# A triangular inverse by doubling: the fine levels kept 32 columns wide per head, with VectorE block transposes in place of TensorE's

## The chip, the cores and the metric

One core of one Trainium2 chip. The metric is the device time of one execution in microseconds (us), the median of several runs.

## What is computed

The program runs two transformer blocks on 256 tokens of width 1024: a first block with mixture-of-experts weights (most of the time), and a second one with forgetting attention and a gated delta rule. The change lies in the delta rule. The reference solves, per head and chunk, a unit lower triangular system:

```
A = jnp.where(tri_strict, einsum(kb, kc) * decay, 0.0)
lhs = A + jnp.eye(C)
sol = lax.linalg.triangular_solve(lhs, concatenate([vc * bc, kb * exp(gc)]), lower=True, unit_diagonal=True)
```

The kernel works with chunks of 128 tokens (two chunks, `t` = 0, 1), 8 heads in two groups of four (`hg` = 0, 1, `HG` = 4), all in 32-bit floats. Instead of solving, it builds the inverse of `lhs` itself, and multiplies with it afterwards.

## The kernel before

Everything of interest stands in `phase_c`, which writes each engine's instructions out by hand, in order, with semaphores between engines. TensorE writes into eight PSUM banks in rotation; the class `Banks` plans which bank each product gets (`banks.plan`, L1852 to L1855), TensorE claims it, the reader takes and releases it, and `banks.moved` waits for such a release.

**The inverse by doubling.** X is the inverse of the block diagonal part of `lhs` with blocks of size 2^l, XT its transpose. Level l joins pairs of blocks: with ATm, the transposed A masked to the off-diagonal squares that level l joins (mask `lm[:, l]`, with a minus sign in it), the step is X <- X + X (A masked) X. Level 0 needs no product. Levels 1 to 6 run in a loop (TensorE L2398 to L2426). One level is, for both chunks t, with four heads each:

- POOL masks A into ATm (L2095), 128x512 numbers per chunk.
- TensorE: t1 = ATm times X, four products of 128x128 by 128x128 (L2407), and from level 2 on a transpose of X, four more (L2413).
- ScalarE copies t1 out of PSUM (L2002) and the transposed X into XT (L2005).
- TensorE: XT times T1, four products (L2425).
- VectorE adds the result to X, at the last level to XT (L2252).

A 32-bit product of 128x128 by 128x128 appears in the trace as two passes, each a weight load (PEld, LDWEIGHTS) and a MATMUL; a transpose is one pass. So a level has 32 passes of products and 8 of transposes.

**What stands around it.** Ahead of the loop VectorE forms XT of level 0 (L2243), TensorE transposes it (`x1`, L2394) and ScalarE copies it to X (L1994). These lie between the projections `fv` and `gz` (`rows`, L1745 to L1752). Behind the loop come the attention logits `lo` (L2436 to L2445) and the products with XT (L2458). Projections run as three products of a high and a low part of the weights; ScalarE makes the high part (L183), VectorE and POOL in turn the low part (L186), four 128x1024 units ahead, in between their other work, where the code says `units.ahead`. SyncE loads a new 2 MB piece of weights into one of two slots once all low parts of the piece two before it are made (L70). POOL also masks the attention weights of the delta rule (L2087), and at the start of the phase it builds the level masks `lm` and other constants, of which `negmask` (L2072) is the last.

Of the kernel before, what the change touches and what calls it, by code (L numbers as in the profile page):

```python
# [31 lines left out]
ALU = mybir.AluOpType  # L32
ACT = mybir.ActivationFunctionType
AX = mybir.AxisListType

P = 128
# [1757 lines left out]
def phase_c(nc, A, sem, sb, ring, banks, k, env):  # L1794
# [20 lines left out]
    ATm, T1 = work[:, 0], work[:, 1]  # L1815
# [27 lines left out]
    for hg in range(2):  # L1843
# [6 lines left out]
                   ("fv", hg, 0), ("fv", hg, 1), *[("x1", hg, t) for t in range(NT)],  # L1850
                   ("gz", hg, 0), ("gz", hg, 1))
        for l in range(1, LEVELS):  # L1852
            for t in range(NT):
                banks.plan(("t1", hg, l, t), *([("tr", hg, l, t)] if l > 1 else []))
            banks.plan(*[("xx" if l < LEVELS - 1 else "xt", hg, l, t) for t in range(NT)])  # L1855
# [12 lines left out]
    with nc.Block() as block:  # L1868
# [18 lines left out]
        def _(act):  # L1887
# [48 lines left out]
            for hg in range(2):  # L1936
# [55 lines left out]
                for t in range(NT):  # L1992
                    bank = banks.take(act, ("x1", hg, t))
                    banks.release(act.copy(X[:, t], heads(bank)), ("x1", hg, t))  # L1994
                for t in range(NT):
# [51 lines left out]
        def _(g):  # L2047
# [6 lines left out]
            for l in range(LEVELS):  # L2054
                if l == 1:
# [10 lines left out]
                                      pattern=[[2 * b, m], [0, b]], channel_multiplier=-1))  # L2066
            mask_plain = vb[:, 0, 0, :]
# [6 lines left out]
            for hg in range(2):  # L2074
                u0 = UNITS_GROUP * hg
                units.ahead(g, "low1", u0 + 20)
                g.wait_ge(sem("kk"), 4 * hg + 4)
                for l in range(LEVELS):
                    if l == 1:
                        units.ahead(g, "low1", u0 + 24)  # L2080
                    if l in (4, 5):
                        units.ahead(g, "low1", u0 + 24 + 2 * (l - 3))
                    if l in (2, 3):

                        for h in (2 * l - 4, 2 * l - 3):
                            banks.moved(g, ("kq", hg, h))
                            g.tensor_tensor(attnT[:, :, h, :], attnT[:, :, h, :],  # L2087
                                            tri[:, :].unsqueeze(1).to_broadcast([P, NT, P]), ALU.mult)\
                                .then_inc(sem("attn_masked"), 1)
                    for t in range(NT):  # L2090
                        if l > 1:
                            banks.done(g, ("t1", hg, l - 1, t))
                        if l == 1:
                            g.wait_ge(sem("x1T"), NT * hg + t + 1)
                        g.tensor_tensor(heads(ATm[:, t, :]), AT[:, t], lm[:, l, :].unsqueeze(1).to_broadcast([P, HG, P]),  # L2095
                                        ALU.mult).then_inc(sem("ATm"), 1)
# [3 lines left out]
        def _(v):  # L2100
# [73 lines left out]
            for hg in range(2):  # L2174
# [65 lines left out]

                for t in range(NT):
                    v.wait_ge(sem("ATm"), 2 * LEVELS * hg + t + 1)
                    v.tensor_tensor(XT[:, t], heads(ATm[:, t, :]), ident[:, :].unsqueeze(1).to_broadcast([P, HG, P]),  # L2243
                                    ALU.add).then_inc(sem("x1T"), 1)
                units.ahead(v, "low0", UNITS_GROUP * hg + 28)
                for l in range(1, LEVELS):
                    for t in range(NT):
                        w, buf = ("xx", X) if l < LEVELS - 1 else ("xt", XT)
                        bank = banks.take(v, (w, hg, l, t))
                        if w == "xt":  # L2250
                            banks.moved(v, ("tr", hg, l, t))
                        banks.release(v.tensor_tensor(buf[:, t], buf[:, t], heads(bank), ALU.add), (w, hg, l, t))  # L2252
# [44 lines left out]
        def _(pe):  # L2297
# [41 lines left out]
            for hg in range(2):  # L2339
# [50 lines left out]
                for t in range(NT):  # L2390
                    pe.wait_ge(sem("x1T"), NT * hg + t + 1)
                    bank = banks.claim(pe, ("x1", hg, t))
                    for h in range(HG):
                        last = pe.transpose(bank[:, h * P:(h + 1) * P], XT[:, t, h, :], ident[:, :])  # L2394
                    banks.filled(last, ("x1", hg, t))
# [403 lines left out]
```

## Time and profile before

| | |
|---|---|
| median of 3 runs | 1648.52 us (1648.29 to 1649.6) |
| the profiled execution | 1648.02 us, its span 1646.3 us |
| TensorE (PE) busy | 99% of the span |
| weight loads (PEld) | 57% |
| VectorE, ScalarE, POOL | 37%, 29%, 18% |
| granted TensorE clock, mean | 0.998 |
| level loop, group 0 / group 1 | 1146.51 to 1174.31 us / 1285.10 to 1312.89 us |

Starts are given in us from the span's start. In a timeline a row's first number is its start, the second its length, and a number in brackets is how long the engine had been idle before it, with what released it. Rows of one line are merged, so that "x8" is eight instructions. The granted clock is a share of full speed: 1.00 is 2.4 GHz, 0.50 is 1.2 GHz. A MATMUL's end is modelled and contains the pipeline's latency, so lengths of MATMULs overlap; the distance between starts tells what one costs.

### The profile page before, as it was taken

The numbers are of one execution on the slowest core, as the hardware profiler recorded it, in microseconds if no ns is written. First come the engines' busy times: TensorE is split into PE (matmuls) and PEld (weight loads), VectorE is DVE, ScalarE is ACT, GpSimd is POOL, SyncE is SP. The second block draws the span as 40 slices with busy tenths as digits, with TensorE's granted clock in tenths as the row PEclk, the third lists the DMA queues.
The fourth block names the chain that finished last, engine by engine and source line by source line (L and its number), as shares of the span: only waits on it lengthen the run. The fifth ranks groups of instructions, "written<-read, shape, count | busy, mean of one in ns | idle before, by whom it ended". The sixth has DMA issues, their size and how long they took to land. (4 is left out here: it accounts for less than half of the span.)

```text
span 1646.3 us, 22758 instructions
## 1 busy us (share of the span) xinstructions
PE 1624.4 (99%) x9272; PEld 946.4 (57%) x9272; DVE 613.7 (37%) x1144; ACT 475.8 (29%) x695; POOL 302.4 (18%) x192
## 2 busy tenths in 40 slices
PE   9999999999999999999999999999999999999998
PEld 8843333333333333333333333698998999999986
DVE  7743212112121212121121211675485244468852
ACT  5421110111111111111011111574555454454443
POOL 3500000000000000000000000535333624445552
PEclk9999999999999999999999999999999999999999
DMA  9698999999999999999999999353133215456552
GB/s 350 221 367 338 428 427 426 428 427 426 428 426 427 429 426 427 426 428 428 428 428 428 428 428 422 125 179 128 53 123 134 103 52 195 166 166 203 167 192 102
DMA packets 92919, 507.67 MB, mean 308 GB/s; under 512 B 8987, under 2 KB 32584, under 8 KB 68264
## 3 DMA queue, kind: packets, MB, share of 16 engines
q1 hardware_dynamic: 92696, 506.00, 76.1%
q8 instruction: 61, 1.00, 0.3%
q10 hardware_dynamic: 144, 0.52, 0.1%
q14 instruction: 18, 0.15, 0.0%
HBM read 505.46 MB, written 1.05 MB: 308 GB/s over the span
## 5 line engine op out<-in xcount | busy, mean ns | idle before, releaser
L186 POOL TENSOR_TENSOR low<-ring,high 128x1024 fp32r<-128x1024 f32 x81 | 199.6, 2465 | 1262.8 <-ACT high L183 1262.7
L1593 PE MATMUL ps<-ring,x 128*64 128x512 f32 x1536 | 337.5, 594 | 1.8 <-DMA ring<-in_w_up 1.8
L1593 PEld LDWEIGHTS ps<-ring,x 128*64 128x64 f32 x1536 | 108.0, 137 | 227.5 <-issue 222.4
L183 ACT CAST high<-ring 128x1024 fp32r<-128x1024 f32 x162 | 168.2, 1047 | 201.4 <-PE ps L1727 125.5
L1720 PE MATMUL ps<-hTh,high 128*128 128x256 f32 x800 | 198.8, 285 | 2.4 <-DVE hTl L633 1.9
L1721 PE MATMUL ps<-hTl,high 128*128 128x256 f32 x800 | 197.6, 284 | 0.0
L1626 PE MATMUL ps<-ring,x 128*64 128x512 f32 x752 | 171.7, 598 | 0.0
L186 DVE TENSOR_TENSOR low<-ring,high 128x1024 fp32r<-128x1024 f32 x81 | 111.1, 1371 | 146.7 <-ACT high L183 146.6
L1720 PEld LDWEIGHTS ps<-hTh,high 128*128 128x128 f32 x800 | 153.9, 192 | 4.2 <-issue 3.8
L1721 PEld LDWEIGHTS ps<-hTl,high 128*128 128x128 f32 x800 | 154.0, 192 | 0.0
L1466 DVE TENSOR_SCALAR hT<-ps 128x512 f32<-128x512 f32 x32 | 22.1, 692 | 295.8 <-PE ps L1593 295.8
L1593 PE MATMUL ps<-extra,x 128*64 128x512 f32 x512 | 113.8, 594 | 0.0
L1727 PE MATMUL ps<-hTh,low 128*128 128x256 f32 x784 | 110.8, 284 | 0.0
L1626 PEld LDWEIGHTS ps<-ring,x 128*64 128x64 f32 x752 | 49.8, 136 | 103.9 <-issue 103.9
L1727 PEld LDWEIGHTS ps<-hTh,low 128*128 128x128 f32 x784 | 101.9, 193 | 0.0
L1418 DVE TENSOR_TENSOR x<-ps,g 128x512 f32<-128x512 f32 x33 | 22.8, 692 | 204.3 <-PE ps L1559 204.3
L1531 ACT COPY hT<-ps 128x512 f32<-128x512 f32 x32 | 18.8, 586 | 261.5 <-PE ps L1626 261.5
L1526 ACT COPY gpickT<-ps 128x256 f32<-128x256 f32 x32 | 11.9, 372 | 251.5 <-PE ps L1606 251.5
L1522 ACT ACTIVATE hT<-hT 128x512 f32<-128x512 f32 x32 | 20.1, 630 | 220.9 <-DVE hT L1466 220.9
L1472 DVE TENSOR_SCALAR hT<-ps 128x512 f32<-128x512 f32 x32 | 22.1, 691 | 155.5 <-PE ps L1593 155.5
L1593 PEld LDWEIGHTS ps<-extra,x 128*64 128x64 f32 x512 | 36.0, 137 | 75.1 <-issue 74.4
L1568 PE MATMUL ps<-hT,gpickT 64*128 64x512 f32 x264 | 65.6, 615 | 0.7 <-ACT hT L1531 0.7
(465 smaller groups left out, 2181.7 us busy)
## 6 DMA issues: line engine op xcount, KB each, us to landing
ring<-in_w_down SPq DMA_DIRECT2D x52, 2048.0 KB, 20.5
ring<-in_w_gate SPq DMA_DIRECT2D x48, 2048.0 KB, 18.2
ring<-in_w_up SPq DMA_DIRECT2D x48, 2048.0 KB, 18.5
ring<-in_w_in SPq DMA_DIRECT2D x23, 2048.0 KB, 8.2
extra<-in_w_gate SPq DMA_DIRECT2D x16, 2048.0 KB, 18.9
extra<-in_w_up SPq DMA_DIRECT2D x16, 2048.0 KB, 17.5
extra<-in_w_down SPq DMA_DIRECT2D x14, 2048.0 KB, 21.0
ring<-in_w_up SPq DMA_DIRECT2D x22, 1024.0 KB, 7.4
```

What stands on the lines that cost most here:

```text
L183: eng.copy(hi, self.raw(u)).then_inc(self.sem("high_split"), 1)
L186: eng.tensor_tensor(lo, self.raw(u), hi.bitcast(F32), ALU.subtract).then_inc(self.sem(who + "_split"), 1)
L1418: bank_free(v.tensor_tensor(xg[:, :, :, :], bank.rearrange("p (c h j) -> p c h j", c=4, h=2), gains, ALU.mult), G_)
L1466: bank_free(v.tensor_scalar(gt[:, :], bank, 7.0, None, ALU.min), GATE)
L1472: bank_free(v.tensor_scalar(up[:, :], bank, 7.0, -7.0, ALU.min, ALU.max), UP)
L1522: act.activation(sg[:, :], gt[:, :], ACT.Sigmoid, scale=1.702).then_inc(sem("sig"), 1)
L1568: last = pe.matmul(total(t, h), gpickT[h * CAP:(h + 1) * CAP, t, :], y[h * CAP:(h + 1) * CAP, :], start=False, stop=final)
L1593: last = pe.matmul(bank[h * CAP:(h + 1) * CAP, :], xg[:, c, kh, :], w[:, c, h * 512:(h + 1) * 512], start=False, stop=kh == 1 and c == 3)
L1626: last = pe.matmul(bank[h * CAP:(h + 1) * CAP, :], aT[:, c, kh, :], w[:, c, h * 512:(h + 1) * 512], start=False, stop=kh == 1 and c == 3)
L1720: pe.matmul(out, wh[:, w], xh[:, c, :], start=c == 0, stop=False)
L1721: last = pe.matmul(out, wh[:, w], xl[:, c, :], start=False, stop=False)
L1727: last = pe.matmul(out, wl[:, c * P:(c + 1) * P], xh[:, c, :], start=False, stop=c == KC - 1)
```

## The change

X keeps, for each head, only 32 columns while the blocks are at most 32 wide (`Xc`, 32 columns per head: row block b of it holds the diagonal 32x32 block b). With that, levels 1 to 4 work on 32 columns per head in place of 128. The product is taken with the full mask `below` of all levels under 5, and what does not belong to level l is masked away on the product by VectorE (`below_c`). XT stays 128 wide (block diagonal) and gets its new blocks from Xc by four VectorE transposes of 32x(4x32) per chunk. Level 5 works on 32 columns, then X is widened to 64 columns (`Xw`), and level 6 writes only the missing quarter of XT: at level 5 VectorE copies, per chunk, twice 32 rows into Xw and twice 32 rows into XT, at level 6 once 64 rows into XT. POOL makes 8 masks per group in place of 14. The `x1` transposes and the ones in the loop (`tr`) are gone.

Buffers and constants:

```
-    ATm, T1 = work[:, 0], work[:, 1]
+    near, far = work[:, 0], work[:, 1]
+    R = 32
+    Xw, Xc, Tc, Tw = X[:, :, :, 0:2 * R], X[:, :, :, 2 * R:3 * R], X[:, :, :, 3 * R:], X[:, :, :, 2 * R:]
+    below = sb("below", [P, P])
+    below_c = sb("below_c", [P, 4, R])
+    odd_row = sb("odd_row", [P, 1])
+    FINE = 5
+    XT_STEPS, AT_STEPS = 4 + NT * (FINE - 1), 8
+    def blocks(odd=None):
+        return [slice(b, b + R) for b in range(R if odd else 0, P, R if odd is None else 2 * R)]
```

ScalarE: no copies of `x1`, `t1` only at levels 5 and 6.

```
-                for l in range(1, LEVELS):
+                for l, to, w in ((FINE, Tc, R), (FINE + 1, Tw, 2 * R)):
                     for t in range(NT):
+                        if l == FINE:
+                            banks.moved(act, ("xx", hg, l - 1, t))
+                            act.copy(Xw[:, t, :, 0:R], Xc[:, t])
+                            act.activation(Xw[:, t, :, R:], Xc[:, t], ACT.Copy, scale=odd_row[:, 0:1])
                         bank = banks.take(act, ("t1", hg, l, t))
-                        banks.release(act.copy(T1[:, t, :], bank), ("t1", hg, l, t))
-                        if l > 1:
-                            bank = banks.take(act, ("tr", hg, l, t))
-                            banks.release(act.copy(XT[:, t], heads(bank)), ("tr", hg, l, t))
+                        last = act.copy(to[:, t], bank[:, 0:HG * w].rearrange("p (h n) -> p h n", h=HG))
+                        banks.release(last, ("t1", hg, l, t))
```

POOL, at the start of the phase, ahead of `negmask`, and per group:

```
+            chain(g.tensor_tensor(below[:, :], lm[:, 0, :], lm[:, 1, :], ALU.add))
+            for l in range(2, FINE):
+                chain(g.tensor_tensor(below[:, :], below[:, :], lm[:, l, :], ALU.add))
...
+                def masked(to, t, mask):
+                    g.tensor_tensor(heads(to[:, t, :]), AT[:, t], mask.unsqueeze(1).to_broadcast([P, HG, P]), ALU.mult)\
+                        .then_inc(sem("ATm"), 1)
+                for t in range(NT):
+                    masked(far, t, lm[:, 0, :])
+                for t in range(NT):
+                    masked(near, t, below[:, :])
+                units.ahead(g, "low1", u0 + 24)
+                for t in range(NT):
+                    g.wait_ge(sem("x1T"), XT_STEPS * hg + 2 * t + 1)
+                    masked(far, t, lm[:, FINE, :])
+                for h in range(HG):
+                    banks.moved(g, ("kq", hg, h))
+                    g.tensor_tensor(attnT[:, :, h, :], attnT[:, :, h, :],
+                                    tri[:, :].unsqueeze(1).to_broadcast([P, NT, P]), ALU.mult)\
+                        .then_inc(sem("attn_masked"), 1)
+                for t in range(NT):
+                    banks.done(g, ("t1", hg, FINE - 1, t))
+                    masked(near, t, lm[:, FINE + 1, :])
+                units.ahead(g, "low1", u0 + 28)
```

VectorE (levels 5 and 6 as told above):

```
+                if hg == 0:
+                    v.wait_ge(sem("consts2"), 1)
+                    for rows in blocks():
+                        v.transpose(below_c[rows, :, :], lm[rows, 1:FINE, rows])
+                    chain(v.tensor_reduce(odd_row[:, :], lm[:, FINE, :], AX.X, ALU.add))
+                    chain(v.tensor_scalar(odd_row[:, :], odd_row[:, :], 1.0 / R, 1.0, ALU.mult, ALU.add))
                 for t in range(NT):
-                    v.wait_ge(sem("ATm"), 2 * LEVELS * hg + t + 1)
-                    v.tensor_tensor(XT[:, t], heads(ATm[:, t, :]), ident[:, :].unsqueeze(1).to_broadcast([P, HG, P]),
+                    v.wait_ge(sem("ATm"), AT_STEPS * hg + t + 1)
+                    v.tensor_tensor(XT[:, t], heads(far[:, t, :]), ident[:, :].unsqueeze(1).to_broadcast([P, HG, P]),
                                     ALU.add).then_inc(sem("x1T"), 1)
+                    v.wait_ge(sem("x1T"), XT_STEPS * hg + 2 * t + 1)
+                    for rows in blocks():
+                        last = v.transpose(Xc[rows, t], XT[rows, t, :, rows])
+                    last.then_inc(sem("x1T"), 1)
                 units.ahead(v, "low0", UNITS_GROUP * hg + 28)
-                for l in range(1, LEVELS):
+                def fine(bank):
+                    return bank[:, 0:HG * R].rearrange("p (h n) -> p h n", h=HG)
+                for l in range(1, FINE):
                     for t in range(NT):
-                        w, buf = ("xx", X) if l < LEVELS - 1 else ("xt", XT)
-                        bank = banks.take(v, (w, hg, l, t))
-                        if w == "xt":
-                            banks.moved(v, ("tr", hg, l, t))
-                        banks.release(v.tensor_tensor(buf[:, t], buf[:, t], heads(bank), ALU.add), (w, hg, l, t))
+                        bank = banks.take(v, ("t1", hg, l, t))
+                        last = v.scalar_tensor_tensor(Tc[:, t], fine(bank), -1.0,
+                                                      below_c[:, l - 1, :].unsqueeze(1).to_broadcast([P, HG, R]),
+                                                      ALU.mult, ALU.mult)
+                        banks.release(last, ("t1", hg, l, t))
+                    for t in range(NT):
+                        bank = banks.take(v, ("xx", hg, l, t))
+                        banks.release(v.tensor_tensor(Xc[:, t], Xc[:, t], fine(bank), ALU.add), ("xx", hg, l, t))
+                        banks.moved(v, ("xx", hg, l, t))
+                        for rows in blocks():
+                            last = v.transpose(XT[rows, t, :, rows], Xc[rows, t])
+                        last.then_inc(sem("x1T"), 1)
```

TensorE:

```
                 for l in range(1, LEVELS):
+                    left, n = (near, 2) if l < FINE else (far, 4) if l == FINE else (near, 6)
+                    right, w = (Xc, R) if l <= FINE else (Xw, 2 * R)
                     for t in range(NT):
-                        pe.wait_ge(sem("ATm"), 2 * LEVELS * hg + 2 * l + t + 1)
+                        pe.wait_ge(sem("ATm"), AT_STEPS * hg + n + t + 1)
                         if l == 1:
-                            banks.moved(pe, ("x1", hg, t))
+                            pe.wait_ge(sem("x1T"), XT_STEPS * hg + 2 * t + 2)
                         else:
                             banks.moved(pe, ("xx", hg, l - 1, t))
                         bank = banks.claim(pe, ("t1", hg, l, t))
                         for h in range(HG):
-                            last = pe.matmul(bank[:, h * P:(h + 1) * P], ATm[:, t, h * P:(h + 1) * P], X[:, t, h, :],
+                            last = pe.matmul(bank[:, h * w:(h + 1) * w], left[:, t, h * P:(h + 1) * P], right[:, t, h, :],
                                              start=True, stop=True)
                         banks.filled(last, ("t1", hg, l, t))
-                        if l > 1:
-                            bank = banks.claim(pe, ("tr", hg, l, t))
-                            for h in range(HG):
-                                last = pe.transpose(bank[:, h * P:(h + 1) * P], X[:, t, h, :], ident[:, :])
-                            banks.filled(last, ("tr", hg, l, t))
                     for t in range(NT):
                         banks.moved(pe, ("t1", hg, l, t))
-                        if l > 1:
-                            banks.moved(pe, ("tr", hg, l, t))
-                        w = "xx" if l < LEVELS - 1 else "xt"
-                        bank = banks.claim(pe, (w, hg, l, t))
-                        for h in range(HG):
-                            a, b = XT[:, t, h, :], T1[:, t, h * P:(h + 1) * P]
-                            if w == "xt":
-                                a, b = b, a
-                            last = pe.matmul(bank[:, h * P:(h + 1) * P], a, b, start=True, stop=True)
-                        banks.filled(last, (w, hg, l, t))
+                        if l <= FINE:
+                            if l > 1:
+                                pe.wait_ge(sem("x1T"), XT_STEPS * hg + 4 + NT * (l - 2) + t + 1)
+                            bank = banks.claim(pe, ("xx", hg, l, t))
+                            for h in range(HG):
+                                last = pe.matmul(bank[:, h * R:(h + 1) * R], XT[:, t, h, :], Tc[:, t, h, :],
+                                                 start=True, stop=True)
+                            banks.filled(last, ("xx", hg, l, t))
+                        if l == FINE:
+                            bank = banks.claim(pe, ("xt", hg, l, t))
+                            for b in (0, 2 * R):
+                                for h in range(HG):
+                                    last = pe.matmul(bank[b:b + R, h * R:(h + 1) * R], Tc[:, t, h, :],
+                                                     XT[:, t, h, b + R:b + 2 * R], start=True, stop=True)
+                            banks.filled(last, ("xt", hg, l, t))
+                        if l > FINE:
+                            banks.moved(pe, ("xt", hg, FINE, t))
+                            bank = banks.claim(pe, ("xt", hg, l, t))
+                            for h in range(HG):
+                                last = pe.matmul(bank[0:2 * R, h * w:(h + 1) * w], Tw[:, t, h, :], XT[:, t, h, 2 * R:],
+                                                 start=True, stop=True)
+                            banks.filled(last, ("xt", hg, l, t))
```

## Rows read from the trace of the kernel before

**Rows 1.** The page, busy time of each engine over the whole span.
```profile
PE 1624.4 (99%) x9272; PEld 946.4 (57%) x9272; DVE 613.7 (37%) x1144; ACT 475.8 (29%) x695; POOL 302.4 (18%) x192
```
**Rows 2.** Busy time by stretch: PE, PEld, DVE, ACT, POOL, clock, DMA share, GB/s.
```profile
1146.51:1174.31 27.80, 27.35 (x235) 26.70 (x233) 7.57 (x12) 13.79 (x26) 18.51 (x14) 1.00 0.22 77
```
**Rows 3.** Timeline of level 3 of group 0: start, length, engine, line.
```profile
1155.70 0.97 PEld L2407 LDWEIGHTS ps<-X,work 128*128 128x128 f32 x8
...
1156.90 0.59 ACT L2002 COPY work<-ps 128x512 f32<-128x512 f32 x1 [2.21 <-PE ps L2407]
...
1158.36 1.98 PEld L2425 LDWEIGHTS ps<-work,XT 128*128 128x128 f32 x16
...
1159.56 0.69 DVE L2252 TENSOR_TENSOR X<-X,ps 128x512 f32<-128x512 f32 x1 [2.92 <-PE ps L2425]
...
1160.32 0.97 PEld L2407 LDWEIGHTS ps<-X,work 128*128 128x128 f32 x8
```
**Rows 4.** Timeline, the x1 transposes of group 0 and the next weight load.
```profile
1134.73 1.03 PEld L2394 LDWEIGHTS ps<-ident,XT 128*128 128x128 f32 x8
...
1135.73 0.19 PEld L1745 LDWEIGHTS ps<-high,hTh 128*128 128x128 f32 x1
```
**Rows 5.** Timeline of the router: products with 32 moving columns, and a reader.
```profile
119.70 0.52 PEld L1274 LDWEIGHTS ps<-fold,part_sums 128*128 128x128 f32 x4 [1.01 <-ACT part_sums L843]
...
120.44 0.22 DVE L1048 TENSOR_TENSOR lg<-ps,brt 128x64 f32<-128x64 f32 x1 [2.44 <-PE ps L1274]
...
123.82 0.30 PEld L1285 LDWEIGHTS ps<-mask,ones 128*128 128x128 f32 x2
...
124.04 0.30 PEld L1286 LDWEIGHTS ps<-mask,ustrict 128*128 128x128 f32 x2
...
124.39 0.09 PEld L1287 LDWEIGHTS ps<-mask,ones 128*1 128x1 f32 x2
```
**Rows 6.** Groups of instructions by line and shape: busy in all, mean ns of one.
```profile
L990 DVE TENSOR_TENSOR extra<-ps,extra 128x128 f32<-128x128 f32 x4 | 1.1, 273 | 0.0
L2087 POOL TENSOR_TENSOR xn<-xn,tri 128x256 f32<-128x256 f32 x8 | 5.7, 734 | 0.0
```
**Rows 7.** Timeline of VectorE: one pair with a wait between, one without.
```profile
1177.78 0.41 DVE L2257 TENSOR_REDUCE fmax<-ps 128x1 f32<-128x256 f32 x1
1178.22 0.17 DVE L2258 TENSOR_SCALAR fmax<-fmax 128x2 f32<-128x2 f32 x1
...
1181.58 0.28 DVE L2262 TENSOR_SCALAR work<-work,fsum 128x128 f32<-128x128 f32 x1
1181.78 0.35 DVE L2263 TENSOR_SCALAR work<-work,fsum 128x256 f32<-128x256 f32 x1
```
**Rows 8.** Timeline: low-part splits and the products that wait for them, a load.
```profile
1065.16 4.75 POOL L186 TENSOR_TENSOR low<-ring,high 128x1024 fp32r<-128x1024 f32 x2
...
1070.10 0.28 PE L1727 MATMUL ps<-hTh,low 128*128 128x256 f32 x1
...
1128.71 1.21 DVE L186 TENSOR_TENSOR low<-ring,high 128x1024 fp32r<-128x1024 f32 x1
...
1130.84 2.40 POOL L186 TENSOR_TENSOR low<-ring,high 128x1024 fp32r<-128x1024 f32 x1 [3.36 <-ACT high L183]
...
1137.67 0.62 PE L1752 MATMUL ps<-low,hTh 128*128 128x512 f32 x2
...
1162.10 0.37 SPq L70 DMA_DIRECT2D ring<-in_w_in  x1
```
**Rows 9.** Busy time by stretch around 1245 us (columns as in rows 2).
```profile
1241.90:1245.30 3.40, 3.40 (x18) 2.48 (x18) 2.16 (x8) 3.38 (x5) 0.39 (x1) 0.99 0.53 149
1245.30:1248.70 3.40, 3.40 (x19) 3.40 (x18) 2.50 (x4) 3.39 (x10) 0.00 (x0) 0.51 1.05 405
```
**Rows 10.** Timeline, TensorE in these two stretches.
```profile
1242.15 0.18 PEld L2367 LDWEIGHTS ps<-row_high,sel 8*128 8x128 f32 x1 [0.76 <-issue]
...
1246.77 1.82 PEld L1727 LDWEIGHTS ps<-hTh,low 128*128 128x128 f32 x8
...
```

More of the change, by code:

```diff
@@ L1849, in phase_c @@
                    *[(w, hg, t) for w in ("kt", "vt") for t in range(NT)],
-                   ("fv", hg, 0), ("fv", hg, 1), *[("x1", hg, t) for t in range(NT)],
+                   ("fv", hg, 0), ("fv", hg, 1),
                    ("gz", hg, 0), ("gz", hg, 1))
         for l in range(1, LEVELS):
+            banks.plan(*[("t1", hg, l, t) for t in range(NT)])
             for t in range(NT):
-                banks.plan(("t1", hg, l, t), *([("tr", hg, l, t)] if l > 1 else []))
-            banks.plan(*[("xx" if l < LEVELS - 1 else "xt", hg, l, t) for t in range(NT)])
+                banks.plan(*[(w, hg, l, t) for w in (["xx"] * (l <= FINE) + ["xt"] * (l >= FINE))])
         banks.plan(*[("lo", hg, h) for h in range(HG)], ("u0", hg), ("wT", hg), ("st", hg), ("o0", hg), ("u1", hg),
@@ L1992, in _ @@
                 for t in range(NT):
-                    bank = banks.take(act, ("x1", hg, t))
-                    banks.release(act.copy(X[:, t], heads(bank)), ("x1", hg, t))
-                for t in range(NT):
                     ahead(u0 + 24 + (3, 4)[t])
@@ L2077, in _ @@
                 g.wait_ge(sem("kk"), 4 * hg + 4)
[L2078 to L2090, printed above, removed]
-                        if l > 1:
[L2092 to L2096, printed above, removed]
+                def masked(to, t, mask):
[18 more added lines that the diff above has]
+                units.ahead(g, "low1", u0 + 28)
             units.ahead(g, "low1", UNITS_E + 11)
@@ new lines, in _ @@
+                for t in range(NT):
+                    bank = banks.take(v, ("xx", hg, FINE, t))
+                    for rows in blocks(True):
+                        last = v.tensor_copy(Xw[rows, t, :, 0:R], fine(bank)[rows])
+                    banks.release(last, ("xx", hg, FINE, t))
+                    bank = banks.take(v, ("xt", hg, FINE, t))
+                    for b in (0, 2 * R):
+                        last = v.tensor_copy(XT[b:b + R, t, :, b + R:b + 2 * R], fine(bank)[b:b + R])
+                    banks.release(last, ("xt", hg, FINE, t))
@@ L2254, in _ @@
+                for t in range(NT):
+                    bank = banks.take(v, ("xt", hg, FINE + 1, t))
+                    wide = bank[0:2 * R, 0:HG * 2 * R].rearrange("p (h n) -> p h n", h=HG)
+                    banks.release(v.tensor_copy(XT[0:2 * R, t, :, 2 * R:], wide), ("xt", hg, FINE + 1, t))
                 for h in range(HG):
@@ L2389, in _ @@
                 both_t(u0 + 20, "fv", hg)
-                for t in range(NT):
-                    pe.wait_ge(sem("x1T"), NT * hg + t + 1)
-                    bank = banks.claim(pe, ("x1", hg, t))
-                    for h in range(HG):
-                        last = pe.transpose(bank[:, h * P:(h + 1) * P], XT[:, t, h, :], ident[:, :])
-                    banks.filled(last, ("x1", hg, t))
                 both_t(u0 + 24, "gz", hg)
                 for l in range(1, LEVELS):
+                    left, n = (near, 2) if l < FINE else (far, 4) if l == FINE else (near, 6)
+                    right, w = (Xc, R) if l <= FINE else (Xw, 2 * R)
                     for t in range(NT):
-                        pe.wait_ge(sem("ATm"), 2 * LEVELS * hg + 2 * l + t + 1)
+                        pe.wait_ge(sem("ATm"), AT_STEPS * hg + n + t + 1)
                         if l == 1:
-                            banks.moved(pe, ("x1", hg, t))
+                            pe.wait_ge(sem("x1T"), XT_STEPS * hg + 2 * t + 2)
                         else:
@@ L2415, in _ @@
                     for t in range(NT):
                         banks.moved(pe, ("t1", hg, l, t))
-                        if l > 1:
-                            banks.moved(pe, ("tr", hg, l, t))
-                        w = "xx" if l < LEVELS - 1 else "xt"
-                        bank = banks.claim(pe, (w, hg, l, t))
-                        for h in range(HG):
-                            a, b = XT[:, t, h, :], T1[:, t, h * P:(h + 1) * P]
-                            if w == "xt":
-                                a, b = b, a
-                            last = pe.matmul(bank[:, h * P:(h + 1) * P], a, b, start=True, stop=True)
@@ new lines, in _ @@
+                        if l == FINE:
+                            bank = banks.claim(pe, ("xt", hg, l, t))
+                            for b in (0, 2 * R):
+                                for h in range(HG):
[9 more added lines that the diff above has]
+                            banks.filled(last, ("xt", hg, l, t))
```

## The prediction

> **What bounds the kernel now.** I read the page first: TensorE is busy for 99% of the span, every other engine for 37% or less [rows 1]. The reader should take from it that time goes only where TensorE's own work shrinks, or where it is made to wait. Then the stretches of the two level loops: 27.80 us each (1146.51 to 1174.31, and the same again in group 1), TensorE busy 27.35 of them, clock 1.00, VectorE 7.57, ScalarE 13.79 [rows 2]. Then the timeline of one level [rows 3]: weight loads start at 1155.70, the second round of products at 1158.36, the next level at 1160.32, so a level takes 4.62 us. It has 40 passes (32 of products, 8 of transposes), 0.115 us each: the loop is bound by TensorE's passes and hardly by its waits. From the start of a group of eight passes to its reader on another engine are 1.20 us (1158.36 to 1159.56), from a reader's end to TensorE 0.07 (1160.25 to 1160.32) [rows 3].
>
> **What the change takes from TensorE.** The eight x1 transposes cost 1.00 us (1134.73 to 1135.73) [rows 4]: minus 1.0 per group. The eight transposes per level would be 0.9 us. The products of levels 1 to 4 move 32 columns in place of 128, but that makes them no shorter: in the router, two passes with 128 columns of weights and 32 moving columns stand 0.22 us from the next two (the 0.30 us that two loads last overlap) [rows 5], the same 0.11 per pass, so the weight load sets the price. The way to the reader is no shorter either: four such passes from 119.70, reader at 120.44 [rows 5], 0.44 and 0.30, so 1.2 for eight. Only products with few weight columns are cheap: two loads of one column take 0.09 together [rows 5]. So the floor of a fine level is 32 x 0.11 = 3.55 us.
>
> **What it puts on VectorE.** Per level VectorE masks t1 (two), adds (two) and makes eight block transposes, in the order mask, mask, add, four transposes, add, four transposes. An operation on 128 numbers per lane out of PSUM takes 0.27 [rows 6]; I take 0.28. No row shows a block transpose. It too moves 128 numbers per lane. From below: the distance between two instructions without a wait is 0.20 (1181.58 to 1181.78). From above: full length and a wait, 0.28 + 0.03 (1177.78 + 0.41 to 1178.22 is 0.03) [rows 7]. I take 0.32: a transpose has to read a whole block before it can write, and the overlap in the rows is between instructions that all begin on lane 0, which these do not.
>
> The Trainium skill (VectorE: DVE Perf Modes, section "Two Vector instructions with no wait between them") says that an instruction whose operands begin in another group of 32 partitions than the last one's starts only when all earlier ones have ended. No row here shows it; by it the four transposes would each cost their full length, by the overlap rule of the rows 0.20, and it speaks against this change.
>
> **A fine level at full clock.** From the start of the second round for chunk 0: 1.20 to the reader, add 0.28, wait 0.04, four transposes 4T, add 0.28, wait 0.04, 4T, mask 0.28, 0.06 to TensorE, which starts the next second round. That is 2.18 + 8T: 4.74 us with T = 0.32, 3.78 with T = 0.20, against 4.62 before. So the saved transposes are eaten by VectorE, and what is late next is its mask behind the second chunk's transposes.
>
> **The whole loop at full clock.** Level 1 reaches its second round after 16 passes, 1.8. Three levels of 4.74: 16.0. Level 5's second t1 waits for the second add (1.20 + 0.28 + 0.04 + 1.28 + 0.28 + 0.06 = 3.1) and ends at 20.0; then per chunk 8 passes (0.9) and 16 with 32 weight columns at 0.05 (0.8): 23.4. Level 6: 16 passes 1.8, 16 with 64 weight columns at 0.06 to 0.11, 1.0 to 1.8: 26.2 to 27.0. ScalarE's copies of 128 or 256 numbers and VectorE's of 32 rows (0.3 to 0.45 each) lie beside these passes. Against 27.8 that is minus 1.2, with x1 minus 2.2 per group. With T = 0.20 it is minus 5.5 per group.
>
> **What stays hidden, and by what.** VectorE's first eight block transposes and, in group 0, its set-up (four transposes, a reduce, a scale, 1.9) come ahead of the low-part split at 1128.71: 4.5 later it would end at 1134.5, and TensorE asks for it at 1137.67, less 1.0 [rows 8]. POOL's two new early masks (2.5) fit into its 3.36 of waiting ahead of 1130.84 [rows 8]. Without these covers TensorE would wait up to 4.5 and 2.5. POOL's four additions at the start of the phase push the two splits at 1065.16 back: 128 numbers per lane, under the 0.73 that 256 take [rows 6]; at 0.5 each the first split would end at 1069.6, and TensorE asks at 1070.10 [rows 8]. I take 0, with 0.6 as the dear end. The last two low splits of POOL move behind its mask for level 6, so the load issued at 1162.10 [rows 8] comes 3 to 15 us later; its slot is read only in the second projection of the next group, over 30 us on, and a load takes some 8. Nothing.
>
> **The clock.** Around 1245 us the granted clock fell from 1.00 to 0.51 (the lower level, 1.2 GHz) for 3.4 us [rows 9]. What TensorE did before: eight products that use 8 of its 128 rows, and two short gaps, one of 0.76 [rows 10]; the record still calls it busy for 3.40 of 3.40 us [rows 9]. So what keeps the clock up is not the busy record but how much of the array works. The fine levels are thin in just that sense: each 0.11 us pass moves 32 columns where it moved 128, and TensorE has gaps of over a microsecond per level besides. The rows of before hold no such stretch, so a fall cannot be read there; I think it the likeliest thing. The price at the lower level: the eight passes at 1246.77 take 1.82 [rows 10], 0.22 each.
>
> The Trainium skill (TensorE: Matmul & The Clock Gate, section "Part 1: The HAM clock gate") says that the slow clock is the default and that activity releases it. The fall at 1245 agrees that it is given by activity, and rows alone do not say whether loading weights counts as such. If it did, the first rival below would hold.
>
> **The sum.** With the clock at 0.5 a fine level is bound by its passes, 32 x 0.22 = 7.0 us, and VectorE is hidden. The clock should fall some 4 to 6 us into the loop. Level 1 and the start of level 2 at full clock, 4.6 (3.6 and nine passes more); the rest of levels 2 to 4, 21.0 less nine passes at 0.22, 19.0: 23.6. Level 5: 32 passes with full weights 7.0, 32 narrow ones at 0.06, 1.9: 32.5. Level 6, where work gets wider and the clock may be back: 16 at 0.11 to 0.22 and 16 at 0.06 to 0.11, 3 to 5. About 36.5 us against 27.8: plus 8.7; x1 minus 1.0: 7.7 per group, 15 in all; an open end behind the loop of up to 1.5 per group is left to the range. The profiled execution has 1648.02 us (span 1646.3), 0.5 under the median of 1648.52; 1648.0 + 15 = **1663**. The likeliest case's own range is 1655 (clock falls late, returns at level 5: 3.5 per group) to 1671 (11 to 11.5 per group).
>
> **The rivals.**
> *The clock stays, VectorE's chain is short.* For it: weight loads keep the array at work in every pass, and TensorE is still recorded busy. Against it: rows 9. Levels take 3.8 to 4.7: minus 2.2 to minus 5.5 per group, 4 to 11 in all, centre 1643. It decides as long as T is under 0.4.
> *The clock stays, the block transposes are dear.* At T = 0.42 the loop costs what the 2.2 per group bring (24 x 0.1 = 2.4), and the time is 1648; at 0.5 it is 1652. Nothing in the rows shows a 128-number operation so long.
> *The change does not shorten TensorE's work at all*, since narrow products cost the same: true for products, but x1 and the loop's transposes do go, so only the second rival yields no change.
>
> **How the numbers follow.** Clock falls: 0.68, 1663. Clock stays, short chain: 0.25, 1643. Clock stays, dear transposes: 0.07, about 1649. A measurement of this kernel can tell about 0.2%, 3.3 us. Slower: 0.68 and a third of the last case, 0.70; same: 0.05; faster: 0.25. The likeliest case alone would leave out three in ten, so the range reaches down to 1640, which takes most of the first rival, and up to 1670.
>
> **What would show it.** The granted clock in the stretch from 5 us into each level loop to its end: 0.5 means the forecast, 1.00 a rival. Loops of 36 to 39 us, TensorE without idle time there, weight loads of the fine levels 0.22 apart. If the clock holds: second rounds 4.7 apart with TensorE waiting for VectorE's transposes, and single transposes 0.32 apart; 0.20 would mean 3.8. The x1 passes must be gone, and TensorE must not wait for the splits near 1070 and 1137. The forecast is wrong if the clock stays at 1.00, and its size is off if the clock falls only now and then.

## The result, and the profile after

The changed kernel takes 1677.58 us, median of 4 runs (1676.76 to 1678.28), against 1648.40 (1648.05 to 1649.6) for the kernel before: ratio 1.0176, 95% interval [1.0161, 1.0192], 29 us slower. The forecast was 1663, range 1640 to 1670. Its sign held and the fall of the clock that it named came, but the loss is twice the 15 us that it forecast.

The page of the kernel after:

```profile
span 1675.5 us, 22761 instructions
PE 1654.1 (99%) x9240; PEld 973.3 (58%) x9240; DVE 644.4 (38%) x1258; ACT 455.3 (27%) x663; POOL 292.9 (17%) x184
PEclk9999999999999999999999999997799599999999
```

The share of TensorE is the same 99% as before [rows 1]: this row cannot tell the two kernels apart. The clock row can: three of its 40 slices stand at 7, 7 and 5.

Busy time by stretch of the kernel after (length, then PE, PEld, VectorE, ScalarE, POOL, granted clock, DMA share, GB/s). The first three are the level loop of group 0 while the clock still holds, its rest, and the attention logits behind it; the fourth is the whole loop; the last is the slow stretch of group 1:

```profile
1146.02:1150.68 4.66, 4.66 (x42) 4.62 (x40) 2.22 (x9) 2.08 (x4) 1.38 (x2) 1.00 0.29 105
1150.68:1184.00 33.32, 33.08 (x185) 32.51 (x184) 14.90 (x50) 2.37 (x8) 7.14 (x4) 0.50 0.19 63
1184.00:1194.87 10.87, 10.87 (x33) 8.07 (x33) 2.61 (x9) 3.00 (x9) 0.00 (x0) 0.50 0.01 2
1146.02:1184.00 37.98, 37.74 (x226) 37.13 (x224) 17.12 (x58) 4.46 (x12) 8.52 (x6) 0.56 0.20 69
1304.28:1348.65 44.37, 44.34 (x217) 40.82 (x217) 17.37 (x60) 6.18 (x21) 7.14 (x4) 0.50 0.13 48
```

Against the one row of before [rows 2]: the loop takes 37.98 us in place of 27.80, with TensorE busy for 37.74 of them and the clock at 0.50 from 4.66 us in. And the clock stays there past the end of the loop. The logits, from 1184.00 until the products with XT at 1194.87, take 10.87 us. In the kernel before they took 5.84 at clock 1.00:

```profile
1174.31:1180.15 5.84, 5.84 (x32) 4.46 (x32) 2.39 (x9) 3.00 (x9) 0.00 (x0) 1.00 0.02 4
```

In all the clock is at 0.50 from 1150.68 to 1195.05, 44.37 us, and for just as long in group 1. The account of group 0 is: loop plus 10.2, logits plus 5.0, and the loop starts 0.5 earlier, 14.7 in all. That of group 1 is: loop plus 10.1 (1298.87 to 1336.73, 37.86 in place of 27.79), logits plus 5.0 (1336.73 to 1347.60), and the way from the logits of group 0 to this loop 0.9 shorter (104.0 in place of 104.9), 14.2 in all. Together that is 28.9 of the 29.2 between the two spans (1675.5 less 1646.3). One short fall of 3.4 us stands in both executions, near 1245 before [rows 9] and near 1260 after, and drops out.

Timeline of the weight loads of the kernel after, from the end of level 1 to the end of the logits:

```profile
1147.92 1.87 PEld L2463 LDWEIGHTS ps<-X,XT 128*128 128x128 f32 x16
1149.70 0.97 PEld L2453 LDWEIGHTS ps<-X,work 128*128 128x128 f32 x8
1151.00 1.78 PEld L2453 LDWEIGHTS ps<-X,work 128*128 128x128 f32 x8 [0.32 <-issue]
1152.66 3.53 PEld L2463 LDWEIGHTS ps<-X,XT 128*128 128x128 f32 x16
...
1159.49 0.76 PEld L2463 LDWEIGHTS ps<-X,XT 128*128 128x128 f32 x3
...
1166.32 3.53 PEld L2463 LDWEIGHTS ps<-X,XT 128*128 128x128 f32 x16
1169.73 3.53 PEld L2453 LDWEIGHTS ps<-X,work 128*128 128x128 f32 x16
1173.14 1.83 PEld L2463 LDWEIGHTS ps<-X,XT 128*128 128x128 f32 x8
1175.03 0.74 PEld L2470 LDWEIGHTS ps<-XT,X 128*32 128x32 f32 x16
...
1178.49 3.49 PEld L2453 LDWEIGHTS ps<-X,work 128*128 128x128 f32 x16
1182.10 1.78 PEld L2477 LDWEIGHTS ps<-XT,X 128*64 128x64 f32 x16
1184.00 0.28 PEld L2489 LDWEIGHTS ps<-row_high,sel 8*128 8x128 f32 x1
...
1189.71 0.28 PEld L2489 LDWEIGHTS ps<-row_high,sel 8*128 8x128 f32 x1 [0.65 <-issue]
...
1194.87 1.18 PEld L2511 LDWEIGHTS ps<-vb,XT 128*128 128x128 f32 x8
```

Two groups of eight loads side by side show the fall: 0.97 us at 1149.70, 1.78 at 1151.00. From there the second rounds of levels 2, 3 and 4 start 6.83 us apart (1152.66, 1159.49, 1166.32), with loads back to back: 32 passes at 0.21. VectorE is ready long before it is asked. Level 5 begins at 1169.73, level 6 at 1178.49, the logits of heads 0 and 1 at 1184.00 and those of heads 2 and 3 at 1189.71.

### The profile page after: what moved, and what is told of

Its sections match the earlier page's. It is cut to its first block and busy times, and to the rows that moved or that the text cites. A ratio compares the mean times of both kernels' runs of the same rounds, so it can differ in the third digit from the quotient of the medians.

```text
span 1675.5 us, 22761 instructions
## 1 busy us (share of the span) xinstructions
PE 1654.1 (99%) x9240; PEld 973.3 (58%) x9240; DVE 644.4 (38%) x1258; ACT 455.3 (27%) x663; POOL 292.9 (17%) x184
## 3 DMA queue, kind: packets, MB, share of 16 engines
HBM read 505.46 MB, written 1.05 MB: 302 GB/s over the span
```

## The experiments

Seven kernels ran. Experiments 2, 3, 5 and 7 were executed once, the others four to six times. Each is compared with the kernel before on the same chip (1648.26 for the first four, 1648.19 for the last three). A difference of a few us between single executions need not come from an edit: short falls of the clock such as that near 1245 come and go, and in experiment 1 the quickest execution (1641.62) has a mean clock of 0.999 and the slowest (1644.8) one of 0.997.

### 1. The same change, with products that move 128 columns

```
-                            last = pe.matmul(bank[:, h * w:(h + 1) * w], left[:, t, h * P:(h + 1) * P], right[:, t, h, :],
+                            n_rep = P // w if l > 0 else 1
+                            src = right[:, t, h, :]
+                            if n_rep > 1:
+                                src = src.unsqueeze(1).to_broadcast([P, n_rep, w])
+                            last = pe.matmul(bank[:, h * w * n_rep:(h + 1) * w * n_rep], left[:, t, h * P:(h + 1) * P], src,
```

The same for the second product, L2463, and readers that take the first copy of each head. The products `xt` (L2470, L2477), with 32 or 64 columns of weights, stay narrow. Instructions, waits and data are those of the changed kernel.

> Edit: in every product of levels 1 to 6 whose moving side is 32 or 64 columns (t1 and xx), the same columns are moved four (two) times, 128 in all, into a bank of 128 columns per head; the readers take the first 32 (64). Nothing else. Theory A (the clock fell because each pass moves too few columns): granted clock 1.00 in both loops and behind them; loops of 26.2 to 27.0 us in place of 37.98, the stretch behind them back from 10.9 to 5.8 us; second rounds 4.7 us apart, because VectorE's eight transposes of 0.31 are in the chain; 1643 to 1646 us in all, 2 to 5 under the kernel before. Rival B (the clock fell because TensorE waits for VectorE in every level): the waits stay, so the clock falls all the same, 1674 to 1680 us. Rival C (the time has nothing to do with the clock, but with VectorE's chain): 1675 us too, with the clock up.

Measured: 1643.74 us, median of 6 (1641.62 to 1644.8), ratio to before 0.997 [0.9958, 0.9982]. Busy time by stretch (loop and logits of group 0, columns as above):

```profile
1145.38:1171.93 26.55, 24.28 (x227) 22.51 (x225) 16.84 (x58) 4.46 (x12) 8.54 (x6) 1.00 0.19 64
1171.93:1177.80 5.87, 5.87 (x34) 4.49 (x33) 2.17 (x9) 3.00 (x9) 0.00 (x0) 1.00 0.41 150
```

Timeline: the second round of level 1, then from the second round of level 2 to that of level 3:

```profile
1147.28 1.87 PEld L2472 LDWEIGHTS ps<-X,XT 128*128 128x128 f32 x16
...
1149.06 0.97 PEld L2458 LDWEIGHTS ps<-X,work 128*128 128x128 f32 x8
...
1152.03 1.86 PEld L2472 LDWEIGHTS ps<-X,XT 128*128 128x128 f32 x16 [0.62 <-DVE X L2280]
1153.55 1.25 DVE L2289 STREAM_TRANSPOSE XT<-X 32x128 f32<-32x128 f32 x4
1156.78 0.30 PEld L2472 LDWEIGHTS ps<-X,XT 128*128 128x128 f32 x2 [0.62 <-DVE X L2280]
```

The transposes as a group by shape (busy in all, mean ns of one, idle before):

```profile
L2289 DVE STREAM_TRANSPOSE XT<-X 32x128 f32<-32x128 f32 x32 | 9.7, 303 | 0.6
```

The clock is 1.00 through the loop and the logits, and 34 us come back (1677.58 to 1643.74) though the widened products move two to four times as many columns. So the fall hangs on the width of what moves. Repeating columns costs TensorE nothing here: the second round of level 1, which ran at clock 1.00 in both kernels, takes 1.78 us for its sixteen passes with 32 columns (1147.92 to 1149.70 in the changed kernel) and 1.78 with 128 (1147.28 to 1149.06), 0.111 each. What is left is the change as it works at full clock: a loop of 26.55 us, in which TensorE is busy for 24.28 and its loads wait 0.62 per level for VectorE's mask. All is as expected.

### 2. The kernel before, with narrow products

```
-                            last = pe.matmul(bank[:, h * P:(h + 1) * P], ATm[:, t, h * P:(h + 1) * P], X[:, t, h, :],
+                            n = 32 if l < 5 else P
+                            last = pe.matmul(bank[:, h * P:h * P + n], ATm[:, t, h * P:(h + 1) * P], X[:, t, h, 0:n],
```

The same in L2425. All else is as before: the transposes, the waits, the readers. The kernel leaves out 96 of the 128 columns of these products.

> Edit to the kernel before: the products of levels 1 to 4 move only the first 32 columns per head (the other 96 are left out of the computation, readers read the bank as before); passes, transposes, copies and waits as before. Theory A: narrow passes alone pull the clock down though TensorE has no waits: 0.5 from 4 to 6 us into each loop until levels 5 and 6 with their 128 columns bring it back; loop 27.8 becomes 38 to 43 us, 1668 to 1680 us in all. Rival B: no new waits, so the clock stays, 1648 us.

Measured: 1674.94 us, 26.7 over the kernel before, with a loop of 41.49 us in each group (27.80 before). Both are within the range expected. Busy time by stretch:

```profile
1151.22:1181.94 30.72, 30.72 (x148) 30.72 (x148) 5.50 (x8) 8.20 (x14) 14.94 (x12) 0.50 0.20 69
1301.41:1332.13 30.72, 30.72 (x149) 30.72 (x149) 5.50 (x8) 7.90 (x14) 15.37 (x12) 0.50 0.20 69
```

Narrow products alone, in a loop whose transposes still move 128 columns and whose levels 5 and 6 are wide, hold the clock at 0.50 for 30.72 us per group. TensorE has a load in flight in every one of them, and ahead of the fall its loads wait once, for 0.64 us in level 1, as they do in the kernel before at clock 1.00. So neither gaps in its work nor VectorE's new chain are needed for a fall. The same run shows what TensorE did before the clock rose:

```profile
1174.26 3.46 PE L2427 MATMUL ps<-work,XT 128*128 128x32 f32 x16
1177.53 2.05 PE L2408 MATMUL ps<-X,work 128*128 128x128 f32 x8
...
1182.38 2.07 PE L2427 MATMUL ps<-work,XT 128*128 128x128 f32 x16
```

Level 5, the first with 128 moving columns in every pass, begins at 1177.53, and at 1181.94, 4.4 us later, the clock is back. Together with experiment 1 this shows what makes the clock fall in the loop: products whose moving side is narrow.

### 3. Only one of the two products wide

Experiment 1 with t1 wide and the second product (L2472) narrow.

> Edit: as e1, but only t1 moves 128 columns; xx moves 32. Theory A: in between; if half of the passes are enough the clock stays at 1.00 and the time is that of e1, 1643 to 1646 us; if not it falls in some part, up to 1676. I expect that it stays up for part of the loop: 1646 to 1665. Rival B: clock falls, 1674 to 1680 us.

Measured: 1644.77 us. Busy time by stretch, the only slow one of group 0:

```profile
1154.78:1158.19 3.41, 3.41 (x18) 3.41 (x18) 2.87 (x10) 0.00 (x0) 0.00 (x0) 0.50 0.00 0
```

One such stretch of 3.4 us per group, and the loop takes 26.60 us, as in experiment 1: TensorE waits for VectorE there anyway, so the stretch costs nothing that shows. With 32 and 128 columns in turn the clock still falls once per loop, but is back 3.4 us later. The time is 1 us from experiment 1, whose runs spread over 3, and that is not to be read. It lies under the 1646 to 1665 that was thought likeliest, in the 1643 to 1646 of the case that half of the passes suffice.

### 4. Wide at levels 1 to 4 only

Experiment 1 with levels 5 and 6 narrow again. This asks whether the narrow end of the loop loses the clock alone, and whether the logits get it back.

> Edit: as e1, but only levels 1 to 4 move 128 columns; levels 5 and 6 move 32 and 64 as in the changed kernel. It separates the two parts of the loss: the loop, and the stretch behind it in which the clock stayed low. Theory A: clock 1.00 in levels 1 to 4; the last 7 to 10 us of the loop are thin, so the clock falls towards their end, and the attention logits behind them run at 0.5 for 3 to 7 us; 1648 to 1660 us. Rival B: as the changed kernel, 1675 us.

Measured: 1661.34 us, median of 4 (1658.79 to 1661.43), ratio 1.0072 [1.0057, 1.0088]. Busy time by stretch:

```profile
1145.50:1166.80 21.30, 18.95 (x163) 17.73 (x163) 14.13 (x49) 3.65 (x9) 8.14 (x6) 1.00 0.06 21
1166.80:1187.28 20.48, 20.48 (x106) 17.16 (x104) 5.70 (x21) 4.47 (x15) 0.26 (x1) 0.50 0.30 103
```

Timeline of the weight loads, from level 6 on:

```profile
1169.93 3.49 PEld L2458 LDWEIGHTS ps<-X,work 128*128 128x128 f32 x16
...
1175.43 0.28 PEld L2498 LDWEIGHTS ps<-row_high,sel 8*128 8x128 f32 x1
...
1186.30 1.56 PEld L2520 LDWEIGHTS ps<-vb,XT 128*128 128x128 f32 x8
```

The clock falls at 1166.80, in level 5, and comes back at 1187.28, when the products behind the logits have begun. So levels 5 and 6, 8.6 us in experiment 1 (1163.31 to 1171.93), take 12.1 (1163.30 to 1175.43), and the logits 10.87 (1175.43 to 1186.30) in place of 5.87. That is plus 8.5. In group 1 the clock falls later in level 5, the two levels take 11.1 (1308.65 to 1319.73) and the logits again 10.87: plus 7.5. The 16 are most of the 17.6 measured against experiment 1. Half of the loss of the changed kernel needs no narrow product in the fine levels: the end of the loop and the logits do it too. The time is 1.3 over the range expected, since the logits ran at 0.50 for all of their 10.87 us, where 3 to 7 were expected.

### 5. All block transposes on one group of lanes

Experiment 1 with the four transposes reading and writing lanes 0 to 31 only:

```
                         for rows in blocks():
-                            last = v.transpose(XT[rows, t, :, rows], Xc[rows, t])
+                            last = v.transpose(XT[0:R, t, :, rows], Xc[0:R, t])
```

Number and size are the same. The blocks of the other lanes are left out of the computation.

> Edit to e1_wide: the four block transposes of a chunk all read and write lanes 0 to 31 (the blocks of the other lanes are left out of the computation), same number and size. It measures what makes a transpose cost 0.31 us. If an instruction on other lanes than the last one's has to wait for its end (the Trainium skill's rule in VectorE: DVE Perf Modes, section 'Two Vector instructions with no wait between them'), these four overlap and start 0.20 us apart, four end after 0.9 in place of 1.25; second rounds 3.8 to 3.9 apart in place of 4.75, 1636 to 1639 us. If 0.31 is simply what a transpose takes, four still take 1.25 and the time is e1's, 1643 to 1645 us.

Measured: 1635.26 us, 0.7 under the range expected. Timeline:

```profile
1149.34 0.88 DVE L2289 STREAM_TRANSPOSE XT<-X 32x128 f32<-32x128 f32 x4
...
1151.54 1.86 PEld L2472 LDWEIGHTS ps<-X,XT 128*128 128x128 f32 x16
...
1155.25 0.30 PEld L2472 LDWEIGHTS ps<-X,XT 128*128 128x128 f32 x2
```

Four transposes take 0.88 in place of 1.25 us: they start 0.19 apart in place of 0.31. Levels stand 3.71 apart in place of 4.75, which is nearly the 3.55 of its passes. So part of the 0.31 is that each transpose begins on other lanes than the one ahead of it. The Trainium skill (VectorE: DVE Perf Modes, section "Two Vector instructions with no wait between them") says that an instruction whose operands start in another group of 32 lanes than the last one's starts only when all earlier ones have ended. The trace agrees: a transpose lasts 0.303, and the next starts 0.31 behind it on other lanes and 0.19 on the same ones.

### 6. One transpose for all lanes, the placement on ScalarE

Experiment 1, but one VectorE instruction transposes all sixteen 32x32 blocks of a chunk's four heads into a compact buffer (columns of X that hold nothing during these levels), and four ScalarE copies put them in place in XT. Nothing is left out. The lines below show ScalarE's part for levels 1 to 3; that of level 4 is the same but for the level number.

```
-                        for rows in blocks():
-                            last = v.transpose(XT[rows, t, :, rows], Xc[rows, t])
-                        last.then_inc(sem("x1T"), 1)
+                        v.transpose(X[:, t, :, 0:R], Xc[:, t]).then_inc(sem("xtc"), 1)
...
+                        act.wait_ge(sem("xtc"), NT * (FINE - 1) * hg + NT * (l - 1) + t + 1)
+                        for rows in blocks():
+                            last = act.copy(XT[rows, t, :, rows], X[rows, t, :, 0:R])
+                        last.then_inc(sem("x1T"), 1)
```

> Edit to e1_wide: VectorE transposes the blocks of all 128 lanes with one instruction into a compact buffer, and ScalarE, idle in these levels, copies the four blocks into XT (four copies of 32 lanes by 128). VectorE's chain per level falls from 4.75 to 2 adds, 2 transposes, 2 masks; TensorE's 32 passes of 0.11 become the bound. Theory A: second rounds 3.6 to 4.0 us apart, loop 22.5 to 24.5 us, clock 1.00, 1636 to 1640 us. Against it: ScalarE's copies may each take 0.3 with no overlap, 1.2 per chunk and 2.4 per level, and come late for the second round: then 4.2 to 4.6 apart, 1641 to 1644 us.

Measured: 1638.19 us, median of 5 (1635.7 to 1638.63), ratio to before 0.9937 [0.9924, 0.9951]. Busy time of the loop:

```profile
1145.89:1169.07 23.18, 22.88 (x227) 22.07 (x225) 9.94 (x34) 13.69 (x44) 8.49 (x6) 1.00 0.17 58
```

Timeline, from the second round of level 2 to the start of level 3:

```profile
1151.37 1.87 PEld L2480 LDWEIGHTS ps<-X,XT 128*128 128x128 f32 x16
...
1152.89 0.31 DVE L2298 STREAM_TRANSPOSE X<-X 128x128 f32<-128x128 f32 x1
1153.15 1.87 PEld L2466 LDWEIGHTS ps<-X,work 128*128 128x128 f32 x16
1153.24 1.85 ACT L2012 COPY XT<-X 32x128 f32<-32x128 f32 x6 [1.12 <-DVE X L2298]
```

This is as expected. The loop is bound by TensorE's passes again: loads back to back, 22.88 of 23.18 us busy, against 24.28 of 26.55 in experiment 1. The second rounds of levels 2 and 3 start 3.57 us apart (1151.37 and 1154.94), in place of 4.75. It is the best version of the study that leaves nothing out, 10 us under the kernel before and 39 under the changed one.

### 7. Wide work between the loop and the logits

The changed kernel with four products of a constant, 256 columns each, between loop and logits. Their result is not read.

```
+                keep_busy(pe, banks.claim(pe, ("lo", hg, 0)), ones, 4)
                 for j in range(2):
```

> Edit to the changed kernel (narrow passes kept): four products of a constant, 256 columns wide and using all 128 rows, 0.43 us each at full clock, are put between the level loop and the attention logits. It asks what keeps the clock low for the 11 us behind the loop: theory A, that the logits' first products, on 8 rows, are too thin to bring it back. Then the clock returns 3 to 7 us after the dummies begin, the stretch of the logits falls from 10.9 to 6 to 9 us, and the dummies cost 1.7 to 3.4 per group: 1672 to 1679 us in all, with the low stretches ending 4 to 8 us earlier relative to the logits. If the clock simply needs a fixed time, it stays low through the logits and the time is 1684 us.

Measured: 1673.68 us. Timeline of the weight loads:

```profile
1184.66 3.06 PEld L306 LDWEIGHTS ps<-ones 128*128 128x128 f32 x8
1188.38 0.26 PEld L2490 LDWEIGHTS ps<-row_high,sel 8*128 8x128 f32 x1 [0.65 <-issue]
...
1194.32 0.85 PEld L2512 LDWEIGHTS ps<-vb,XT 128*128 128x128 f32 x6
```

Busy time by stretch:

```profile
1184.66:1188.57 3.91, 3.91 (x10) 2.72 (x10) 0.42 (x1) 0.00 (x0) 0.00 (x0) 0.50 0.00 0
1188.57:1195.50 6.93, 6.93 (x41) 5.50 (x42) 2.83 (x12) 3.56 (x12) 0.00 (x0) 1.00 0.01 2
```

The added work takes 3.7 us, a little more than the 3.4 expected at most, and the clock is back just behind its end (1188.57). The logits then take 5.9 us (1188.38 to 1194.32) and keep the clock, where they took 10.87. Net that is 1.2 us per group won, 2.4 of the 3.9 measured. The rest is no doing of the edit: from the logits of group 0 to the loop of group 1 this execution takes 102.6 us in place of 104.0, without the short fall near 1260, and it starts its first loop 0.7 later, with a short fall near 42. So the logits do not lose the clock within their 5.9 us, and whoever comes to them at 0.50 pays 5 us. Whether their last products help to bring it back is not shown: in the changed kernel it was back 0.18 us behind them in group 0 and 1.05 in group 1, in experiment 4 0.98.

## Why the prediction was right in its cause and wrong in its size

**What bounds the kernel.** Right. TensorE's passes, and their price is the weight load: 0.11 to 0.12 per pass at full clock whether 32 or 128 columns move (experiment 1 against the changed kernel's level 1 and [rows 3]), 0.21 to 0.22 at the lower level.

**The clock (forecast: falls 4 to 6 us into the loop, 0.68).** Right in cause and place. It fell 4.66 us into the loop of group 0 and 5.41 into that of group 1 (1298.87 to 1304.28). The reason drawn from [rows 9, 10], that the busy record does not say what keeps the clock up, held: TensorE was recorded busy for 33.08 of the 33.32 slow us, and width alone undoes it. But these rows were thin ground for the rest. The products ahead of that fall use few rows and move 512 columns, so they say nothing of narrow ones; and in experiments 5 and 6 the same instructions ran with the clock at 1.00 throughout. That the moving side is what counts, and not gaps, which the prediction named besides, was shown only by experiments 1 and 2. Experiment 1 has the gaps and keeps the clock; experiment 2 has no more of them than the kernel before and loses it. The Trainium skill (TensorE: Matmul & The Clock Gate, section "Part 1: The HAM clock gate") has activity release the slow clock; the rows agree only if loading weights is not counted as activity, for loads were in flight for 32.51 of the 33.32 us.

**The loop at 0.50 (forecast 36.5 us, plus 8.7).** Step by step: level 5 was to begin 23.6 us into the loop and began at 23.7 (1169.73); level 6 at 32.5 and began at 32.5 (1178.49). Then the forecast gave level 6 "3 to 5" us, 4 in the sum, "where work gets wider and the clock may be back". It took 5.5 (1178.49 to 1184.00), which is its price at 0.50 throughout: 3.6 and 1.9. So the loop was 1.5 short (1.4 in group 1), all of it in that term.

**Behind the loop (forecast "an open end of up to 1.5 per group", left out of the sum).** This is the step that failed: a term put at nothing in the sum. It measured 5.0 per group (10.87 less 5.84), a third of the whole loss. The prediction itself took the eight-row products of [rows 10] for work too thin to keep the clock up, and four such products open each half of the logits. It did not ask which work stands behind the narrow levels and whether that would end the fall. It doesn't: the logits ran at 0.50 from their first product to their last, in the changed kernel and in experiment 4.

**x1 (forecast minus 1.0 per group).** The first loop starts 0.5 earlier. Part of what lacks is ahead of the phase: the profiled execution reaches its first product, L521, 0.25 us later than that of before (1044.72 against 1044.47), and experiment 1, with the same code there, reaches it at 1044.26, so this is spread between executions. By this mark the saving is 0.7 in the run of after and 0.9 in experiment 1 (1146.51 less 1145.38, less 0.21). In group 1, counted from the logits of group 0, it is 0.9 in both. So the term was right to 0.1 to 0.3. The covers held: set-up, masks and the splits near 1065 and 1128 cost nothing that shows.

**VectorE's transposes (forecast 0.32 apart, full-clock level 4.74, loop 26.2 to 27.0).** Right. They measured 0.31 apart, a level 4.75 and a loop 26.55 in experiment 1, and 0.19 apart and 3.71 in experiment 5, where 0.20 and 3.78 were the low end. Of the two reasons given for 0.32 the one from the lanes is what experiment 5 bears out. The other, that a transpose reads a whole block before it writes, does not keep transposes on the same lanes 0.31 apart. In the changed kernel none of it shows, since its levels are bound by slow passes.

**The rivals.** The first, clock kept and chain short, had 1643; the kernel that keeps the clock on the chip measures 1643.7. It was a true picture of the change without its fault. The dear transposes (0.42 or more each) didn't come.

**The sum.** What was missing: the loops 1.5 and 1.4, behind the loops 5.0 each, x1 0.5 and 0.1, 13.5 in all. That is the distance from plus 15.4 (twice 7.7) to the 28.9 accounted for above. The fall of the clock was priced well inside the levels that the change narrowed, and not behind them. The range ended at 1670, from 11 to 11.5 per group, since its dear end held 1.5 for the open end and not 5.

## What to carry to other kernels

Making products narrower can cost time though each takes no longer at full clock: look at the granted clock of the stretch, not at the busy share. Where the weight load sets the price anyway, try moving 128 columns by repeating the same ones, as experiment 1 did. When you forecast a fall of the clock, price it until work arrives that a row shows to bring the clock back, past the end of the stretch that you changed. Where data allow, spread one VectorE instruction over all lanes rather than issue four on a quarter each (experiment 6).

## What the runs showed that was not expected

- Thin products have two sides. The logits ran at 1.00 for their 5.9 us where they met that clock (experiments 1 and 7), and at 0.50 for all of their 10.9 us where they met that (after, experiment 4).
- The short fall of [rows 9] comes and goes. It stands behind the same instructions before, after and in experiment 1, and not in experiments 5 and 6. What decides it is not shown.
- Sixteen transposes by one VectorE instruction of 128x128 take 0.31 us (experiment 6), as long as four blocks on 32 lanes (0.303): here the other lanes came free.
- With every second round of passes wide the clock was low for 3.4 us per group (experiment 3); in experiment 2, where only the transposes are wide, a fifth of a level's passes, for 30.72.
- How wide a product must be was not tried between 32 and 128 columns, nor whether the weights' depth alone (eight rows) would lose the clock.
